# Second layer's feed-forward up-projection as seven block products, with sums of weights on GpSimd and sums of sources on VectorE

## What is computed

```python
h = h + mx[5] * conv_ffn(modulate(rmsnorm(h, norm2_g[l]), mx[3], mx[4]), w_up[l], conv_w[l], conv_b[l], w_down[l])
```

## Time and profile before

| what | value |
|---|---|
| median of 3 runs | 2558.67 us (2556.18 to 2562.14) |
| the profiled execution: span, from first to last instruction | 2559.7 us |
| its own time beside the span | none is listed; the span lies inside the three runs |
| PE busy | 2436.9 us, 95% |
| DVE busy | 1330.9 us, 52% |
| ACT busy | 840.4 us, 33% |
| POOL busy | 304.3 us, 12% |

### The profile page before, as it was taken

The page is one execution under the profiler, slowest core; times in us unless marked ns, Lnnn a source line. Parts: engine busy times, 40 slices in busy tenths (PEclk is TensorE's granted clock), DMA queues, the critical chain, the costliest instruction groups (busy, mean ns, idle before and its releaser), DMA issues. The chain is left out here.

```text
span 2559.7 us, 35115 instructions
## 1 busy us (share of the span) xinstructions
PE 2436.9 (95%) x14850; PEld 1898.1 (74%) x14850; DVE 1330.9 (52%) x2142; ACT 840.4 (33%) x1346; POOL 304.3 (12%) x246
## 2 busy tenths in 40 slices
PE   6999989999999999999999999998999999999977
PEld 5887568888887888897679999774754579773333
DVE  4323664666667313333757777437657856532223
ACT  3324433333235113324434434224323743420001
POOL 0501420000002000302500000000013020011112
PEclk9999999999999999999999999999999999999999
DMA  6213911111111212224512222430210114359998
GB/s 244 83 61 117 336 54 66 66 52 65 66 66 35 68 58 71 74 75 143 226 66 83 99 85 82 134 107 37 86 34 9 50 66 148 149 230 390 417 409 328
DMA packets 63245, 322.32 MB, mean 126 GB/s; under 512 B 8109, under 2 KB 20397, under 8 KB 31789
## 3 DMA queue, kind: packets, MB, share of 16 engines
q1 hardware_dynamic: 51374, 300.27, 31.9%
q0 software_dynamic: 5696, 12.59, 1.3%
q10 hardware_dynamic: 6016, 7.18, 0.8%
HBM read 315.82 MB, written 12.58 MB: 128 GB/s over the span
## 5 line engine op out<-in xcount | busy, mean ns | idle before, releaser
L2394 PE MATMUL ps<-xn_rounded,ring_rounded 128*128 128x258 f32 (+2 forms) x2816 | 531.7, 311 | 0.0
L1096 PE MATMUL ps<-work_rounded,ring_rounded 128*128 128x512 f32 (+2 forms) x1952 | 514.7, 352 | 5.2 <-PEq L901 3.6
L1096 PE MATMUL ps<-xn_rounded,ring_rounded 128*128 128x512 f32 (+3 forms) x2176 | 512.2, 347 | 0.0
L2394 PEld LDWEIGHTS ps<-xn_rounded,ring_rounded 128*128 128x128 f32 x2816 | 411.8, 189 | 30.9
L1096 PEld LDWEIGHTS ps<-xn_rounded,ring_rounded 128*128 128x128 f32 (+1 forms) x2176 | 351.7, 190 | 54.1 <-issue 0.2
L1096 PEld LDWEIGHTS ps<-work_rounded,ring_rounded 128*128 128x128 f32 x1952 | 321.9, 190 | 61.2 <-issue 5.0
L1096 PE MATMUL ps<-big_rounded,ring_rounded 128*128 128x512 f32 (+1 forms) x1200 | 319.1, 356 | 11.2 <-DVE big_rounded L996 8.7
L996 DVE TENSOR_TENSOR ring_rounded<-ring,ring_rounded 128x2048 fp32r<-128x2048 f32 (+4 forms) x107 | 191.4, 1789 | 237.0 <-ACT ring_rounded L960 236.8
L2394 PE MATMUL ps<-work_rounded,ring_rounded 128*128 128x256 f32 (+1 forms) x1232 | 278.5, 307 | 1.5 <-PEq L901 1.5
L960 ACT ACTIVATE ring_rounded<-ring 128x2048 fp32r<-128x2048 f32 (+4 forms) x107 | 161.0, 1505 | 311.4 <-PE ps L1096 279.1
L1096 PEld LDWEIGHTS ps<-big_rounded,ring_rounded 128*128 128x128 f32 x1200 | 196.9, 189 | 52.3 <-DVE big_rounded L996 10.5
(11 more groups left out here) (459 smaller groups left out, 3169.7 us busy)
## 6 DMA issues: line engine op xcount, KB each, us to landing
ring<-in_stream SPq DMA_DIRECT2D x141, 1024.0 KB, 4.9
big<-in_experts SPq DMA_DIRECT2D x44, 1024.0 KB, 23.7
ring<-in_stream SPq DMA_DIRECT2D x32, 704.0 KB, 4.1
ring<-in_experts SPq DMA_DIRECT2D x17, 1024.0 KB, 27.3
xn<-in_experts SPq DMA_DIRECT2D x15, 1024.0 KB, 15.2
work<-in_experts SPq DMA_DIRECT2D x15, 1024.0 KB, 16.0
big<-in_first_modulation SPq DMA_DIRECT2D x8, 1024.0 KB, 14.9
work<-in_bias ACTq DMA_DIRECT2D x20, 256.0 KB, 4.5
```

Source lines behind the costliest of these rows:

```text
L1096: mm = pe.matmul(out[:, a - u.first:b - u.first], lhs, rhs, start=j == 0 and n == 0 and not u.onto, stop=j == terms - 1 and n == len(passe ...
L2394: mm = pe.matmul(out[:, a:b], ws[:, k, :], x[k][:, a - base:b - base], start=k == 0 and n == 0, stop=k == KT - 1 and n == 2)
```

## The change

The 1024 x 256 weight strip of one feature tile (128 columns of the first half, 128 of the gate half) is cut into four blocks of 512 x 128: A11, A12 (first half), A21, A22 (gate half), the sources into four blocks of 512 features x 258 tokens: B11, B12, B21, B22. With the sums S1 = A21+A22, S2 = S1-A11, S3 = A11-A21, S4 = A12-S2, T1 = B12-B11, T2 = B22-T1, T3 = B22-B12, T4 = B21-T2 (in the variant of Winograd) the two halves of the result come from seven products of 12 matmuls of 258 columns each, 84 a feature tile, 1848 in all, in place of 96 and 2112.

Around the products, for each feature tile: POOL makes S1 to S4 (512 columns each), one of the convolution's additions (`add_side`) and the gate product; ACT and DVE split 3584 columns of weights in place of 2048; ACT copies two partial products (`copy_first`, `copy_fifth`), weighs the centre tap with the bias (`centre`) and one side tap; DVE adds two partial products in PSUM (`make_fourth`, `make_fifth`), evicts twice (514 columns), and makes the other three multiply-adds. The modulation's shift is no longer added by ACT. T1 to T4 and their splits are made during the output projection by ACT and DVE, which also do squares; POOL adds the squares and makes the first strips' sums. The root is made by one ACT instruction in place of a root and a reciprocal on DVE. Four down-projection sources are split ahead in place of nine. In the hyena part two rooms change places. The host packs the strips of this matrix in another order; size and number of the loads are the same.

The new class, cut to its queues:

```diff
+        for i in range(FT + 1):
+            order += [("P1", i), ("P5", i)] if i < FT else []
+            order += [("P3", i - 1)] if i >= 1 else []
+            order += [("P6", i)] if i < FT else []
+            order += [("P4", i - 1)] if i >= 1 else []
+            order += [("P2", i), ("P7", i)] if i < FT else []
...
+    def gpsimd(self, pool):
+        self.add_square(pool, KT - 1)
+        self.sum_s1(pool, 1)
+        self.sum_s2(pool, 1)
+        for i in range(FT + 1):
+            if i + 1 < FT:
+                self.sum_s4(pool, i + 1)
+            if i + 2 < FT:
+                self.sum_s3(pool, i + 2)
+            if 0 <= i - 2:
+                self.gate(pool, i - 2)
+            if i + 2 < FT:
+                self.sum_s1(pool, i + 2)
+            if 0 <= i - 1 < FT - 1:
+                self.add_side(pool, i - 1)
+            if i + 2 < FT:
+                self.sum_s2(pool, i + 2)
+        self.gate_last(pool)
...
+    def scalar(self, act):
...
+        for i in range(FT + 1):
+            if 0 <= i - 2:
+                self.weigh_side(act, i - 2)
+            if 1 <= i < FT:
+                self.copy_first(act, i)
+                self.copy_fifth(act, i)
+            if i + 1 < FT:
+                self.high_a11(act, i + 1)
+            if 0 <= i - 2:
+                self.silu(act, i - 2)
+            if 0 <= i - 1 < FT - 1:
+                self.bias(act, i - 1, 0)
+                self.centre(act, i - 1, 0).then_inc(self.centred.up(), 1)
+            if i + 1 < FT:
+                self.high_s1_s2(act, i + 1)
+            if i < FT:
+                self.high_s4_a22(act, i)
+            if 0 <= i - 1 < FT - 1:
+                self.bias(act, i - 1, 1)
+                self.centre(act, i - 1, 1).then_inc(self.centred.up(), 1)
+            if i + 1 < FT:
+                self.high_a12(act, i + 1)
+                self.high_s3(act, i + 1)
...
+    def vector(self, dve):
...
+        for i in range(FT + 1):
+            if 1 <= i < FT:
+                self.low_s1_s2(dve, i)
+            if i >= 1:
+                self.low_s4_a22(dve, i - 1)
+            if 0 <= i - 2:
+                self.convolve_first(dve, i - 2, 0)
+            if 1 <= i < FT:
+                self.low_s3(dve, i)
+                self.low_a12(dve, i)
+            if i >= 1:
+                self.make_fifth(dve, i - 1)
+            if 0 <= i - 2:
+                self.convolve_first(dve, i - 2, 1)
...
+            if i >= 1:
+                self.evict(dve, i - 1, 0)
+            if 0 <= i - 2:
+                self.convolve_second(dve, i - 2)
+            if i < FT:
+                self.make_fourth(dve, i)
+            if i + 1 < FT:
+                self.low_a11(dve, i + 1)
+            if i >= 1:
+                self.evict(dve, i - 1, 1)
...
+    def low_of(self, dve, value, low, high):
+        return dve.tensor_tensor(low, value, high.bitcast(F32), ALU.subtract).then_inc(self.low_made.up(), 1)
...
+    def make_fourth(self, dve, i):
+        dve.wait_ge(self.done.sem, self.after("P6", i))
+        dve.wait_ge(self.fifth_copied.sem, self.fifth_copied.at(i + 1))
+        dve.tensor_tensor(self.bank_of("d", i), self.bank_of("a", i), self.fifth_kept[i % 2], ALU.add).then_inc(self.partial_summed.up(), 1)
...
+    def sum_s4(self, pool, n):
+        pool.wait_ge(self.sums_made.sem, self.sum_number(n, "S2"))
+        pair = lambda part: self.slot(n, part).rearrange("p (k c) -> p k c", k=2)
+        pool.tensor_tensor(pair(2), pair(1), self.sums(2, 2), ALU.subtract).then_inc(self.sums_made.up(), 1)
...
+    def after_eviction(self, dve, i):
...
+        if i in (1, 3, 5):
+            j = i // 2
+            a = slice(j * 258, (j + 1) * 258)
+            dve.wait_ge(self.squared.sem, self.squared.at(2 * i + 1))
+            settle(dve, dve.tensor_tensor(v["T1"][:, a], v["T3"][:, a], v["B11"][:, a], ALU.subtract), self.vstep)
+            settle(dve, dve.tensor_tensor(v["T2"][:, a], v["B22"][:, a], v["T1"][:, a], ALU.subtract), self.vstep)
+            dve.tensor_tensor(v["T3"][:, a], v["B22"][:, a], v["T3"][:, a], ALU.subtract)
+            dve.tensor_tensor(v["T4"][:, a], v["B21"][:, a], v["T2"][:, a], ALU.subtract).then_inc(self.summed_pair.up(), 1)
+        if i in (2, 4, 6):
+            self.pair_lows(dve, i // 2 - 1)
...
+            self.low_a11(dve, 0)
+            self.low_s1_s2(dve, 0)
...
-            at = (FT + 1) * width
-            rooms = tiles_in(width, self.big[:, at:16384], self.xn, self.big[:, FT * width:at])
-            ahead = (16384 - at) // width
+            rooms = tiles_in(width, self.xn[:, 5632:6144], self.big[:, 14874:15898], self.ring[:, 9728:10240], self.xn[:, 0:5632],
+                             self.big[:, 11778:14850], self.work[:, 4624:5136])
+            ahead = 4
```

More of the change, by code:

```diff
@@ L302, in lay_out @@
     for i, ((name, l), rows, cols) in enumerate(PLAN):
-        stream[i, :, :WIDTH[i]] = pack_strip(x[name][l], rows, cols)
+        pack = pack_blocks if (name, l) == ("w_up", DEPTH - 1) else pack_strip
+        stream[i, :, :WIDTH[i]] = pack(x[name][l], rows, cols)
     out["stream"] = stream
@@ L888, in __init__ @@
         self.done = self.sig("product_done")
-        self.joined = None
+        self.joined = self.seven = None
     def sig(self, name):
@@ L2543, in ffn_down, with arrive_last, release_last @@
         sources, tiles_ahead = self.down_sources(l, width)
-        left = self.up_left
+        left, seven = self.up_left, self.seven
         tiles_ahead = tiles_ahead or UP_TILES_AHEAD
+        def arrive_last(pe, i, j):
+            if j == 0 and i < 4:
+                pe.wait_ge(seven.scaled.sem, seven.scaled.at(2 * FT + (-2, -3, 0, -1)[i]))
+            if i == 0 and j == 0:
+                pe.wait_ge(seven.next_low.sem, seven.next_low.at(tiles_ahead + 1))
+        def release_last(act, k):
+            if k == tiles_ahead:
+                act.wait_ge(self.done.sem, seven.all_done)
+                act.wait_ge(seven.gated.sem, seven.after_gate(FT - 4))
+            if k in (7, 8, 9):
+                seven.tap_last(act, 0, k - 7)
+            if k in (11, 12, 13):
+                seven.tap_last(act, 1, k - 11)
+            if k == 16:
+                seven.silu_last(act)
+            if k in (FT - 3, FT - 2):
+                act.wait_ge(seven.gated.sem, seven.after_gate(k))
+            if k == FT - 1:
+                act.wait_ge(seven.last_gated.sem, seven.last_gated.at(1))
         def arrive(pe, i, j):
@@ L2549, in arrive @@
                 pe.wait_ge(left.evicted, left.all_evicted - (3 - i if i < 2 else 0))
-            if i == 0 and last and j == 0:
-                pe.wait_ge(left.next_low, left.no_low + 1)
-            if i == 0 and not last and j < UP_TILES_AHEAD:
+            if i == 0 and j < UP_TILES_AHEAD:
                 pe.wait_ge(left.next_low, left.no_low + 2 + j)
-            if i == 0 and not last and j == 8:
+            if i == 0 and j == 8:
                 pe.wait_ge(left.next_low, left.no_low + 2 + UP_TILES_AHEAD)
@@ L2560, in release @@
                 act.wait_ge(left.gated, left.all_gated)
[L2561 to L2564, removed]
+            if k in (6, 8, 10):
+                left.tap(act, 1, (k - 6) // 2)
+            if k == 12:
                 left.silu_last(act)
-            if k == (FT - 1 if last else 15):
+            if k == 15:
                 act.wait_ge(left.last_gated, left.last_all_gated)
@@ L2573, in loads @@
             self.load_strips_until(sp, first + 4)
-            sp.wait_ge(left.done, left.all_done)
-            sp.wait_ge(left.last_gated, left.last_all_gated)
+            sp.wait_ge(self.done.sem, seven.all_done)
+            sp.wait_ge(seven.last_gated.sem, seven.last_gated.at(1))
             self.load_features(sp)
```

484 lines of the change are left out of this document (477 added, 7 removed).

## The result

The changed kernel takes 2627.80 us (median of 4 runs, 2625.86 to 2630.34), the one before 2559.30 beside it (4 runs). The ratio is 1.0263, 95% interval 1.0248 to 1.0278: slower, as forecast, but by 68 us and not by 35. That is outside the range of 2572 to 2622.

The account below looks back on a forecast made before the run. The prediction took PE to bound the up-projection before the change and DVE, stopped by POOL, after it. Stage +31, output projection +1.5 and down-projection start +3 made +35 on 2559.7: 2595 us, range 2572 to 2622.

Parts of the forecast that it names:

- the exclusion: DVE instructions with two SBUF inputs and POOL ones reading SBUF stop each other; each POOL instruction stops DVE for 1.08 us.
- forecast beat of 13.5: Up-projection, per tile: DVE's own 8.0 us plus POOL's 6.5, less 0.34 and 0.60 of overlap, gives 13.5 us.
- The walk: Stepping through DVE's queue over one up-projection tile: two of six POOL instructions overlap PSUM work, giving 13.5 us.
- the rival with tight turns: Up-projection: all DVE PSUM work lies under POOL instructions, beat 12.6 to 12.9, total 2577 to 2583 us; chance 13%.
- The loads don't change and are not waited for: Said of the output projection's loads: unchanged by the change and causing no waits, so no time was added.
- the total of 20 beats without stray waits: Up-projection: 20 beats of 13.5, 270, off 7.6 for missing POOL sums, 2.4 for sources split ahead; together 264.8 us.
- Four sources split ahead for the down-projection, 2.4.: Up-projection stage: splitting four down-projection sources ahead adds 2.4 us.
- Last P7, P3, P4 with a short wait, 4.8.: End of the up-projection: the last products P7, P3, P4 and a short wait take 4.8 us.
- Output projection +1.5: Output projection: DVE's work, about 43 us worst, fits just under 45; the last unit's late share adds 1.5 us.
- my 5.5: Start of the up-projection: 36 matmuls and a start take 5.5 us to the first `make_fourth`.
- The clock falls: Up-projection: PE's idle time in each tile brings half clock, beat 14.5 to 15, total 2615 to 2625 us; chance 11%.
- PE stays the bound: Up-projection: POOL holds DVE up by under 2 us a tile, so the kernel gets faster, 2535 us; chance 6%.

Follow-up runs that it names:

- Experiment one: Changed kernel with each of POOL's six instructions a tile replaced by two memsets, their sums, side tap and gate left out: 2561.1 us, ratio 0.9995.
- six: The kernel with the waits moved, plus all six POOL instructions of a tile put on DVE in an order without waits: 2579.8 us, ratio 1.0069.
- experiment five: Changed kernel with source low parts one tile later, last eviction earlier, smaller fillers, and the strip's low part behind the last eviction: 2608.3 us, ratio 1.0180.
- Experiment two: Changed kernel with DVE making the low parts of the four sources split ahead one tile later: 2617.9 us, ratio 1.0214.
- Three: Changed kernel with the output projection's last eviction ahead of the third pair's low parts, and fillers of 260 columns: 2622.9 us, ratio 1.0240.
- eight: Changed kernel with the high-weight by low-source pass left out, 56 matmuls a tile in place of 84: 2618.0 us, ratio 1.0222.

## Why the prediction was right and wrong

**Right: the exclusion and its price.** The forecast beat of 13.5 was 13.1; POOL's instructions took 1.5 to 2.1 us, DVE's 512-column ones up to 1.8. Experiment one removes only the reads and the stretching ends; six removes POOL and the beat is DVE's own work. This is the rule of the Trainium skill that the prediction weighed (SBUF — State Buffer, section "Who interferes with whom"), and experiment one agrees with its other half too: a GpSimd instruction that only writes SBUF did not hold DVE up. The walk put two of six POOL instructions under PSUM work; in the timeline it is three, the third under `make_fourth`, and 6.5 - 0.34 - 0.34 - 0.60 = 5.2 are left (5.6 predicted, 5.1 measured). So the clean beat lies between the forecast's 13.5 and the 12.6 to 12.9 of the rival with tight turns. The forecast that splits of 1024 would be near 2.2 us was wrong in the clean beat: POOL waits 2.51 us there for the strip's load and begins second, so it is POOL's S3 that is held up. The prediction had "The loads don't change and are not waited for"; they don't change, but each beat's S3 waits for one. In the timeline that changes which engine waits there; six DVE instructions are stretched, one for each of POOL's.

**Right by luck: the total of 20 beats without stray waits**, 264.8 us in experiment five, by terms that cancel: shorter beats (13.1), but 14.4 to 14.9 in the tiles with a source split and up to 14.2 in single others.

**Wrong: "Four sources split ahead for the down-projection, 2.4."** That step priced four DVE instructions and not the wait that each brought: I did not follow ACT's queue to the point at which the high part is made. DVE stood idle for 12.6 us in those four tiles, then the next tile ran late, with PE stopped four times (14.5 us) and the clock at 0.50 behind some of the stops. The beats were 276.6 us in place of 264.8. Experiment two, which only moves the four instructions, gives 10 back. In five, what is left over the forecast's stage is 4.7 us: 4.6 more to the first `make_fourth`, 1.3 less to the second, 1.4 more in the tail.

**Wrong: "Last P7, P3, P4 with a short wait, 4.8."** It was 12.6; the strip's low part stood before low S4/A22 and waited 3.1 us for ACT, and PE stood 4.94 us. With it moved the tail is 6.2, at the price of the wait of 3.8 us behind it.

**Wrong: "Output projection +1.5"**, with 1 us for the start inside the 5.5. The sum was off to begin with: 23.2 + 13 + 11 x 1.08 is 48 us and not 43, which is over the projection's 45. Neither is what happened: in the 44.9 us of the projection DVE is busy 30.3. The load was the wrong thing to look at. What counts is what DVE still owes when PE ends, the last pair's splits, for which it first waits 3.10 us for ACT, and the eviction behind them. That and the fillers, which I had not counted, made the border 12.8 us and not 2.3. Three buys 3.5 of the 10.5 back; one, in which POOL reads nothing of the strips, has 3.0 less, so that much of it is the exclusion once more. The first `make_fourth` came 8.9 us after the first product, 3.4 over my 5.5. One needs 6.4: so 2.5 of the 3.4 are the exclusion, on DVE's last splits of sources and first of weights (1.80, 1.77 and 1.49 us in place of 0.68, 0.68 and 0.42). The last 0.9 was not tested.

**How the miss adds up**, in the profiles, over the forecast's terms: beats 11.8, border 9.0, tail 7.8, first `make_fourth` 3.4, second 0.3, the rest of the kernel -3.2; 29 us.

**The rivals.** "The clock falls" gave nearly the right size (2615 to 2625) for a reason that the runs don't bear out: in the clean beats PE is idle 2.0 us in 13.1 and the clock is 0.97, and eight ran at 0.83 and was faster. The low clock comes with the long waits; what it costs on its own was not measured. (Its extreme case, the clock low throughout, is 2749 us by the prediction's own 20 us a tile and not 2740.) "PE stays the bound" is excluded by the beat of 13.1 with DVE in work throughout; even one, without the exclusion, does not reach 2535.

The profiled executions of the changed kernel, of five, six and one, set out along the span as at the top, show how much belongs to which part (difference to before, us):

| | ahead | border | stage | rest | span |
|---|---|---|---|---|---|
| changed | -1.5 | +10.5 | +54.1 | +1.3 | 2624.1 |
| five: waits moved | +2.6 | +6.7 | +35.4 | +2.9 | 2607.2 |
| six: sums on DVE | +0.6 | +6.6 | +6.0 | +6.9 | 2579.8 |
| one: POOL only writes | +0.1 | +7.5 | -6.8 | -0.6 | 2559.8 |

The column "ahead" has the same value already at the projection's first matmul, in code that the three lower rows share with the changed kernel: it is scatter between executions. A part of the larger "rest" of five and six is PE's wait for the moved strip (3.8 and 3.6 us). No version beat the old kernel: the best that computes everything, six, is 0.7% slower. Seven products save PE 1.4 us a tile, but they ask 11.7 us a tile of DVE, and the old beat was 11.52.

## What to carry to other kernels

Fewer matmuls are worth nothing unless the sums that replace them fit beside the work already on the vector engines, and GpSimd is no free engine for them where VectorE's instructions read two inputs from SBUF: add both engines' such work into one queue, and compare that with the beat. A sum may be cheaper on the busier engine (0.61 against 0.85 us of DVE's time here). Then price each instruction in an in-order queue twice, by its duration and by when its input is made: five instructions that take some 5 us in all brought 16 us of idle time on their engine. A load is such an input too: S3 waited for its strip in each beat, which stopped only POOL, and as much as 3.2 us when it stood in DVE's queue.

## What the runs showed of the hardware

- GpSimd memsets of 512 columns, 127 us of them in a stage, left VectorE's two-input instructions at 0.69 and 0.75 us; beside additions of the same size from SBUF their means were 1.51 and 1.32.
- A cover that is too short leaves a remainder: a GpSimd product of 1.28 us placed over 0.94 us of PSUM-reading work held the next SBUF instruction for 0.44 us.
- TensorE idle for 1.73 us once a beat came with a granted clock of 0.97 over four beats; behind an idle time of 3.77 us lie 5.65 us of work at 0.50, 1.2 GHz.
